# Two-layer decoder trunk on one Trainium2 core: the key and query stripes of the first layer multiplied in whole fp32 with the weights stationary, and the gate's rank product moved behind them

## The reference, cut to what matters

```python
mod = cs @ ada_w[l] + ada_b[l]             # six vectors of 2048: shift, scale, gate, twice
h = x * (1.0 + sc_a) + sh_a
proj = h @ w_in                            # q 1024, k 1024, v 2048, r 2048, gl 16 columns
log_a = log_sigmoid(gl @ w_gate_up + b_gate) / 16.0
bc = cumsum(log_a)                         # in chunks of 64 tokens
q_dec, k_intra, k_state = q/16 * exp(bc), k * exp(-bc), k * exp(b_last - bc)
scores = (q_dec @ k_intra.T) * causal      # and the state between chunks
o = rms_norm(scores @ v + state part) * norm_g * silu(r);  y = o @ w_out
x = layer_norm(ALPHA * x + (1.0 + g_a) * y)
```

## Time and profile before

| | us |
|---|---|
| median of 3 runs (range) | 2304.08 (2301.16 to 2308.14) |
| the profiled execution | 2305.37 |
| its span on the core | 2303.6 |
| PE busy | 2237.2 (97%) |
| DVE busy | 1751.9 (76%) |
| ACT busy | 1170.2 (51%) |

### The profile page before, as it was taken

One profiled execution on the slowest core, in us unless ns is written; L12 is line 12 of the kernel. 1 busy time (PEld: TensorE's weight loads), 2 busy tenths in 40 slices (PEclk: granted clock), 3 DMA queues, 4 the chain that ended last, 5 costly groups with the idle time before them and its releaser, 6 DMA issues.

```text
span 2303.6 us, 31826 instructions
## 1 busy us (share of the span) xinstructions
PE 2237.2 (97%) x10900; PEld 1868.7 (81%) x10900; DVE 1751.9 (76%) x1707; ACT 1170.2 (51%) x1445; POOL 18.6 (1%) x42
## 2 busy tenths in 40 slices
PE   5799999999999999999999999999999999999997
...
GB/s 386 377 312 353 364 331 345 323 180 381 375 371 375 376 361 366 334 252 352 304 191 335 287 220 217 303 335 131 302 286 271 189 191 195 224 193 192 192 229 126
DMA packets 146394, 658.14 MB, mean 286 GB/s; under 512 B 16528, under 2 KB 16848, under 8 KB 115712
## 3 DMA queue, kind: packets, MB, share of 16 engines
...
## 4 chain that ended last, share of the span: by engine, by line
PE 89%; DVE 5%; DMA 3%; issue 2%; ACT 1%; SPq 0%; DVEq 0%; ACTq 0%
PE ps L1295 19%; PE ps L1206 18%; PE ps L1207 18%; PE ps L1210 18%; PE ps L1299 10%; DMA R<-in_mods 2%; DVE w_lo L798 1%; DVE mod_w L803 1%; DMA mod_w<-in_mods 1%; DMA raw<-in_tiles 1%; PE ps L1329 1%; PE ps L1316 1%; PE ps L1415 0%; PE ps L1430 0%; DVE R L803 0%
## 5 line engine op out<-in xcount | busy, mean ns | idle before, releaser
L798 DVE TENSOR_TENSOR w_lo<-raw,w_hi 128x1024 fp32r<-128x1024 f32 x756 | 920.9, 1223 | 485.6 <-ACT w_hi L388 482.9
L388 ACT ACTIVATE w_hi<-raw 128x1024 fp32r<-128x1024 f32 x756 | 797.3, 1059 | 857.7 <-PE ps L1210 441.3
L1206 PE MATMUL ps<-w_hi,h_both 128*128 128x512 f32 x2064 | 816.9, 396 | 0.0
L1207 PE MATMUL ps<-w_hi,h_both 128*128 128x512 f32 x2064 | 808.4, 392 | 0.0
L1210 PE MATMUL ps<-w_lo,h_both 128*128 128x512 f32 x2064 | 559.9, 390 | 2.5 <-DVE w_lo L798 2.5
L1295 PE MATMUL ps<-h_both,w_hi 128*128 128x512 f32 x1920 | 480.9, 392 | 0.0
L803 DVE SCALAR_TENSOR_TENSOR mod_w<-mod_w,cs 128x2048 f32<-128x2048 f32 x200 | 457.0, 2285 | 18.8 <-DMA mod_w<-in_mods 11.4
L1206 PEld LDWEIGHTS ps<-w_hi,h_both 128*128 128x128 f32 x2064 | 390.9, 189 | 89.0 <-issue 6.9
L1210 PEld LDWEIGHTS ps<-w_lo,h_both 128*128 128x128 f32 x2064 | 387.9, 188 | 85.8 <-DVE w_lo L798 4.5
L1207 PEld LDWEIGHTS ps<-w_hi,h_both 128*128 128x128 f32 x2064 | 391.1, 189 | 80.7 <-issue 1.0
L1295 PEld LDWEIGHTS ps<-h_both,w_hi 128*128 128x128 f32 x1920 | 345.4, 189 | 61.9
...
## 6 DMA issues: line engine op xcount, KB each, us to landing
...
mod_w<-in_mods SPq DMA_DIRECT2D x200, 1024.0 KB, 6.9
R<-in_mods SPq DMA_DIRECT2D x16, 1024.0 KB, 11.2
R<-in_ln_rows POOLq DMA_DIRECT2D x8, 1024.0 KB, 8.8
...
G<-in_mods SPq DMA_DIRECT2D x4, 1024.0 KB, 11.7
S<-in_mods SPq DMA_DIRECT2D x4, 1024.0 KB, 13.6
G<-g_rows POOLq DMA_DIRECT2D x4, 1024.0 KB, 8.1
```

The lines of the kernel that those rows point to most:

```text
L388: nc.scalar.activation(w_hi[:, slot, :], raw[:, slot, :], ACT.Copy).then_inc(hi_ready, 1)
L798: nc.vector.tensor_tensor(w_lo[:, slot, :], raw[:, slot, :], w_hi[:, slot, :].bitcast(F32), ALU.subtract)\
L1206: mm(dst, h_hi[:, kt, toks], w_hi[:, slot, c], start=start, stop=False, skip_group_check=more)
L1207: return mm(dst, h_lo[:, kt, toks], w_hi[:, slot, c], start=False, stop=False, skip_group_check=more)
```

## The change

The lead takes 4 tiles a pair (32 in all: both key stripes, both query stripes), unsplit: `lead_tile` multiplies `raw` as the stationary operand with the 256 tokens of `xT` moving, both whole fp32, 8 matmuls a tile, into all 8 banks, so that features lie on the partitions. No `w_hi`, `w_lo` is made of them and nothing is turned; ACT copies two banks for each stripe (`cols_out`), and DVE reads those copies. A lead tile's slot is free when PE has used it. The stage gq1 is gone; its four mods stand between lead and gv (`BETWEEN_MODS`). The rank product is one group behind the lead, in split form: weights [hi | lo] of 32 columns, times h_hi and h_lo, 32 matmuls of 256 columns; the 32 result rows meet a doubled `wgu`. The stages get other numbers of mods.

```diff
-_sizes = [("lead", 24), ("gq1", 8), ("gv", 32), ("gr", 32), ("go", 32),
+_sizes = [("lead", 32), ("gv", 32), ("gr", 32), ("go", 32),
...
-LEAD_TILES = 3
+LEAD_TILES = 4
+N_LEAD = LEAD_TILES * KT // 2
...
-SCHEDULE = [("gv", 0, 1, 8), ("gv", 16, 1, 10), ("gr", 0, 2, 8), ("go", 0, 1, 6), ("go", 16, 1, 4), ("u0", 0, 1, 0), ("u0", 16, 7, 8),
+SCHEDULE = [("gv", 0, 1, 4), ("gv", 16, 1, 10), ("gr", 0, 1, 10), ("gr", 16, 1, 8), ("go", 0, 1, 8), ("go", 16, 1, 4), ("u0", 0, 1, 0), ("u0", 16, 7, 8),
...
-HALF_BODY, HALF_BODY_MODS = 8, 4
-PLAN = {T0["gq1"]: (LEAD, HALF_BODY_MODS)}
-_a = LEAD + HALF_BODY_MODS
+BETWEEN_MODS = 4
+PLAN = {}
+_a = LEAD + BETWEEN_MODS
...
-            def load_tile(t, slot, first=False, skipped=0):
-                if not first:
+            def load_tile(t, slot, first=False, skipped=0, unsplit=False):
+                if unsplit:
+                    sp.wait_ge(tile_used, t - RING + 1)
+                elif not first:
                     sp.wait_ge(lo_ready, t - skipped - RING + 1)
...
+                    load_tile(t, t % RING, first=t < RING, unsplit=t >= RING)
+            for i in range(BETWEEN_MODS):
+                load_mod(LEAD + i, i % 2)
...
-                nc.scalar.activation(glT, ps[0:RANK, 6, 0:SEQ], ACT.Copy).then_inc(gl_copied, 1)
-
-            gl_out()
+                nc.scalar.activation(glT, ps[0:2 * RANK, 2, 0:SEQ], ACT.Copy).then_inc(gl_copied, 1)
...
+            def cols_out(i):
+                def f():
+                    act.wait_ge(tile_used, N_LEAD - LEAD_TILES + i + 1)
+                    nc.scalar.activation(gla_cols[i].rearrange("p (a n) -> p a n", a=2), ps[:, 2 * i:2 * i + 2, :], ACT.Copy)\
+                      .then_inc(rows_copied, 1)
+                return f
+
+            for i in range(LEAD_TILES):
+                H[V + i].append(cols_out(i))
+            for at, f in ((3, gl_out), (4, gate_log), (5, gate_log2), (6, gate_log3), (8, decays1), (9, decays2), (10, decays3)):
+                H[V + at].append(f)
+            H[V + 28].append(scores_out)
...
+            def lead_tile(t, pr, i):
+                slot = t % RING
+                pe.wait_ge(raw_loaded[slot], 16 * (t // RING + 1))
+                for k in range(2):
+                    kt = 2 * pr + k
+                    for blk in range(4):
+                        last = mm(ps[:, 2 * i + blk // 2, (blk % 2) * SEQ:(blk % 2 + 1) * SEQ], raw[:, slot, k * SW + blk * P:k * SW + (blk + 1) * P],
+                                  xT[:, kt, :], start=kt == 0 and blk % 2 == 0, stop=kt == KT - 1, skip_group_check=True)
+                last.then_inc(tile_used, 1)
...
-            pe.wait_ge(gl_loaded, 16)
             for pr in range(PAIRS):
-                pe.wait_ge(h_lo_ready, pr + 1)
-                for kt in (2 * pr, 2 * pr + 1):
-                    c = slice(kt * RANK, (kt + 1) * RANK)
-                    last = mm(ps[0:RANK, 6, 0:SEQ], gl_w[:, c], xT[:, kt, :], start=kt == 0, stop=kt == KT - 1)
-                if pr == PAIRS - 1:
-                    last.then_inc(gl_done, 1)
-                for i, bank in enumerate((2, 0, 4)):
-                    t = LEAD_TILES * pr + i
-                    stripe_tile(t, pr, None, slot=t % RING, bank=bank)
+                pe.wait_ge(h_full, pr + 1)
+                for i in range(LEAD_TILES):
+                    lead_tile(LEAD_TILES * pr + i, pr, i)
+
+            def gate_inputs():
+                pe.wait_ge(gl_lo_ready, 1)
+                pe.wait_ge(h_lo_ready, PAIRS)
+                pe.wait_ge(rows_copied, 2)
+                for kt in range(KT):
+                    for n, part in enumerate((h_hi, h_lo)):
+                        last = mm(ps[0:2 * RANK, 2, 0:SEQ], gl_parts[:, kt, :], part[:, kt, :], start=kt == 0 and n == 0, stop=kt == KT - 1 and n == 1)
+                last.then_inc(gl_done, 1)
...
-                pe.wait_ge(rows_copied, 3)
+                pe.wait_ge(rows_copied, 4)
...
-            K, V, RR, O = T0["gq1"], T0["gv"], T0["gr"], T0["go"]
-            H[K + 0].append(gates)
-            for i, copied in enumerate((1, 0, 2, 3)):
-                H[K + 4 * i + 11].append(turn(copied, i, [(gate_sum, 1)] if i == 0 else [(turned_dve, i)], gla_rows[i]))
-            H[V + 20].append(scores)
+            V, RR, O = T0["gv"], T0["gr"], T0["go"]
+            H[V].append(gates)
+            H[V + 25].append(scores)
...
+            gate_inputs()
```

More of the change, by code:

```diff
@@ L233, in token_half @@
             return (rows_buf, turned_buf)[tok][:, pr * SEQ:(pr + 1) * SEQ]
-        HALF_AT = {2 * i: i for i in range(HALF_BODY_MODS)}
+        GV_MODS = {i: i for i in range(4)}
         def mod_positions(per_body):
@@ L268, in load_early, with body @@
                 sp.dma_start(early_raw[:, j, :], tiles[EARLY_AT[e] + j, :, :]).then_inc(early_loaded[j], 16)
-            def body(t, a, per_body, at=None, n=BODY, skipped=0, early=False, ahead=None):
+            def body(t, a, per_body, at=None, skipped=0, early=False, ahead=None, from_lead=False):
                 at = at or mod_positions(per_body)
-                for j in range(n):
+                for j in range(BODY):
                     if not early or j >= EARLY:
-                        load_tile(t + j, j % RING, skipped=skipped)
+                        load_tile(t + j, j % RING, skipped=skipped, unsplit=from_lead and j < RING)
                     if ahead is not None and j in EARLY_LOAD:
@@ L390, in _, with body @@
             H = defaultdict(list)
-            def body(t, hooks=None, lap0=None, early=None, n=BODY):
-                for j in range(n):
+            def body(t, hooks=None, lap0=None, early=None):
+                for j in range(BODY):
                     if early is None or j >= EARLY:
@@ L418, in f @@
                     act.wait_ge(tile_used, done)
-                    if s is not None:
+                    if s:
                         act.wait_ge(blocks_turned, s)
@@ L564, in _ @@
                   .then_inc(xt_copied, 1)
+            act.wait_ge(gl_loaded, 16)
+            nc.scalar.activation(gl_parts[:, :, 0:RANK], gl_w, ACT.Copy).then_inc(gl_hi_ready, 1)
             act.wait_ge(xt_copied, PAIRS)
@@ L790, in link, with split_tile @@
                 dve.wait_ge(dve_step, steps[0])
-            skipped = [0]
-            def split_tile(t, slot, first=False, ring_used=None):
+            skipped = [N_LEAD]
+            def split_tile(t, slot, ring_used=None):
                 dve.wait_ge(hi_ready, t - skipped[0] + 1)
-                if not first:
-                    dve.wait_ge(tile_used, t - RING + 1 if ring_used is None else ring_used)
+                dve.wait_ge(tile_used, t - RING + 1 if ring_used is None else ring_used)
                 nc.vector.tensor_tensor(w_lo[:, slot, :], raw[:, slot, :], w_hi[:, slot, :].bitcast(F32), ALU.subtract)\
@@ L816, in early_hooks, with body @@
                 return {at: [split_early(e, j)] for j, at in enumerate(EARLY_SPLIT)}
-            def body(t, a, lap, per, hooks, early=False, at=None, n=BODY):
+            def body(t, a, lap, per, hooks, early=False, at=None):
                 at = at or mod_positions(per)
-                for j in range(n):
+                for j in range(BODY):
                     if not early or j >= EARLY:
@@ L829, in run @@
                 a, per = PLAN[t]
-                body(t, a, (a - LEAD) // 2, per, {j: H.get(t + j, []) for j in range(BODY)} if hooks is None else hooks, t in EARLY_AT)
+                body(t, a, (a - LEAD) // 2, per, {j: H.get(t + j, []) for j in range(BODY)} if hooks is None else hooks, t in EARLY_AT,
+                     GV_MODS if t == N_LEAD else None)
             def loop(t_first, n, make_hooks):
@@ L988, in _ @@
                     nc.vector.tensor_tensor(coef[:, 1, kts], mod_t[:, a + 2:a + 4], mod_bt[:, a + 2:a + 4], ALU.add).then_inc(lead_coef, 1)
+            for i in range(BETWEEN_MODS):
+                mod_tile(LEAD + i, mod_w[:, i % 2, :], mod_loaded[i % 2], i // 2 + 1)
             g3 = lambda v: v.rearrange("p (j t) -> p j t", j=GJ)
@@ L1075, in _ @@
             H[O + 16 + 10].append(lambda: make_coef(coef, "sc_m0", "sh_m0", 0))
-            body(K, LEAD, 0, None, {j: H.get(K + j, []) for j in range(HALF_BODY)}, at=HALF_AT, n=HALF_BODY)
             for i in range(6):
```

93 lines of the change are left out of this document (38 added, 55 removed).

## The result

The changed kernel takes 2313.72 us (median of 10 runs, 2310.39 to 2319.45) against 2304.70 for the kernel before (10 runs, 2301.16 to 2308.14): a ratio of 1.0043, 95% interval 1.0035 to 1.0051. It is 9.0 us slower where 4 us less were forecast. The profiled execution spans 2311.9 against 2303.6 us, 8.3 more.

What follows compares the result with a forecast made beforehand. PE was taken as full except in the first two slices and the last, with DMA full in the lead. Profiled 2305.4 - 5.1 (seam) + 2 (go) = 2302.3, median 1.3 lower: 2301 us, range 2291 to 2311.

Steps and rivals of the forecast that it cites:

- rival C: Lead: loads of full-row fp32 weights aren't hidden, 5.4 us a tile, 21.6 a pair; total 2340 us; chance 0.05.
- E(p): Lead: the end of PE's pair p, for which SP's next loads wait; PE can begin pair p+2 17.0 to 18.5 later.
- two pairs without a fall: Lead's loop: return way 17.0 to 18.5 us plus 14.1 of PE's own, 31.1 to 32.6, taken as 31.8.
- falls of the clock up to E(6): Lead: PE's clock dropping to 1.2 of 2.4 GHz after idling, 1.5 us each; none taken but at the lead's start.
- E(6): Lead: end of PE's pair 6, put at 40.4 + 3 x 31.8 = 135.8 us; the seam's times count from it.
- V+3 landed, after E(6): Seam: load of value tile 3, behind a chain of mods through two buffers, lands 28.0 us after pair 6 ends.
- `gates` begins, after E(6): Seam: gate matmuls start 30.5 us after pair 6 ends, by PE's way or ACT's, and end at 34.2.
- V+1, slower by: Value tile behind the gate matmuls: the clock is low there as before, costing 1.5 us; V+1 starts at 171.5.
- more in go: Go stage: 8 mods instead of 6, one in slack, one adding DMA time; taken as 2 us, bounds 0 and 5.
- the anchor: Start of tile V+1 with gates behind, where both kernels are compared: 176.6 before, 171.5 after, a gain of 5.1 us.
- Rival B: Lead: clock falls at every pair's start, 1.5 us each; total 2308 us, 2311 with go at its bound; chance 0.15.
- rival D: Seam: mod chain sets V+3 whatever PE does; 1 us more at each of six steps gives 2306 us; chance 0.10.

Runs made afterwards that it cites:

- e1: Changed kernel plus seven zero-weight fp32 matmuls behind lead pairs 1, 3 and 5, so PE doesn't pause; 2310.61 us, 1.0029 of the kernel before.
- e3: Changed kernel with ACT copying the stripes ahead of the value tiles' splits and the rank product behind V+0; 2312.22 us, 1.0033 of the kernel before.
- e6: Changed kernel with the seam's value tiles loaded earlier, between and ahead of mods, and the gate's chain at its old distances; 2309.47 us, 1.0024 of before.
- e5: Changed kernel with each mod load of pair p+2 issued behind one tile of pair p+1; 2301.97 us, 0.9992 of the kernel before.
- e9: Kernel before, each mod load of pair p+2 issued behind one of pair p+1's three tiles, the fourth behind the third; 2297.36 us, ratio 0.9978.

## Why the prediction was wrong

The steps on PE were right: no loads of weights show (rival C is out), a tile takes 3.45 us where 3.52 stood, a pair 13.8 where 14.1. The return way from E(p) to pair p+2 is 16.7 to 16.9 for even p, just under the range of 17.0 to 18.5; for odd p ACT has the pair 18.1 to 18.2 behind E(p), near its upper end. `raw`'s slots are freed by PE, and SP's queue stands behind them, as said. The rest, as the prediction put it:

| step | predicted | trace |
|---|---|---|
| E(0) | 40.4 | 41.8 |
| two pairs without a fall | 31.8 | 16.8 + 14.5 = 31.3 |
| falls of the clock up to E(6) | 0 | 1.7 + 2.9 + 2.9 |
| E(6) | 135.8 | 143.1 |
| V+3 landed, after E(6) | 28.0 | 31.6 |
| rank product, long | 5.3 | 6.5 |
| `gates` begins, after E(6) | 30.5 | 33.8 |
| `gates`, long | 3.7 | 4.8 |
| V+1, slower by | 1.5 | 2.3 |
| more in go | 2 | 0.1 |

The 31.3 is borne out where no fall stands between E(0) and E(2): 31.2 in e1 (41.21 to 72.40), 31.3 in e3, 31.2 in e6. So the loop itself was forecast within 0.5 us.

The step that failed is the sentence **"The new lead leaves about 2 us of idling a pair, between the two rows; I take no fall but at its start."** The mean was about right, 1.5 us a pair. Its form was wrong, and the prediction's own formula had it: if pair p+2 can't begin before E(p) + 16.8 and pair p+1 takes 13.8 gaplessly behind E(p), the whole rest of 3 us stands in front of p+2, none in front of p+1. One hole of 3.4 is next to the 3.36 of the earlier trace rows, whose matmuls ran at half clock. A hole of 1.5 isn't. The price was too low as well: I took 1.5 a fall, from the eight matmuls behind the old `gates`; here it was 1.7 once and 2.9 twice. How many of the holes bring a fall is in part luck: in e3 and e6 the first brought none.

In numbers at V+2's last four matmuls: by the anchor the kernel before would have them at 176.6 + 4.5 = 181.1, the trace of after has them at 188.48, 7.4 later, where 5.1 earlier was said. The 12.5 between are E(6) +7.3 (start +1.4, shorter loop -1.6, falls +7.5), `gates` after E(6) +3.3, its length +1.1, V+1 +0.8 (at full clock the four would stand 2.72 + 1.81 behind the start of V+1, at 181.67 + 4.53 = 186.2, 2.3 earlier), together 12.5. The falls are the largest term. That the program would have been 7.5 us shorter without them is not shown: e1 gave back 3.1, its fillers' cost included. The remaining 0.6 up to u0 I can't place; go was given 2 and took 0.1.

The 3.3 at the seam are the second miss, a matter of size: the chain of mods through two buffers is as told (mods 32 and 33 are at DVE at +5.5 and +8.0, predicted 5.7 and 8.2), but from mod 36 on each lands beside a value tile, and the 4.4 us that I took for a mod alone are 7.5 for mod 38 (issued at 165.93, at DVE at 173.48). That is rival D, with 3.6 us in place of its 6.

Rival B had the mechanism and was given 0.15 and 2308 to 2311. It said that each pair would fall; every second did, for 1.7 to 2.9 us in place of 1.5, and the time is 2.7 us above B's upper end, the seam's miss beside it.

What the runs add to that: the clock kept up with fillers gives back 3.1 us (e1), the order of issue 11.7, the clock's part included (e5), and below both lies the bound of bytes, 15.1 us a pair. It is the cost of the change in the lead that no order takes away: it puts a fourth tile, 0.52 MB, into each of eight pairs, where DMA is full, and takes it out of a stage in which PE was the bound. The lead of e9 has a pair in 13.8 us (107.71 to 121.49), that of e5 in 15.1. I had written that 396 GB/s "is what the lead's DMA bears", but never asked what the order of issues would make of it.
